# Two-pass P·V with the high and low parts of V side by side, in a two-layer mixer kernel

## The chip, the cores and the metric

The kernel runs on one core of one Trainium2 chip. The metric is the device time of one execution in microseconds (us); lower is better. The core's engines work side by side, each through its own queue in order, and wait for each other by semaphores: TensorE (PE in the profile, with its weight loads as PEld), VectorE (DVE), ScalarE (ACT), GpSimd (POOL) and SyncE (SP, which only issues DMAs here).

## The reference

Two layers work on 256 latent tokens (side x) and 256 context tokens (side c) of width 1024. Each layer has four attention branches A, B, C and D of 8 heads with head width 64, gated and merged, then a SwiGLU feed-forward part. What matters here is the last step of every attention:

```python
s = jnp.einsum('bqhgd,bkhd->bhgqk', qi, k, preferred_element_type=jnp.float32) * scale
p = jax.nn.softmax(s, axis=-1)
return jnp.einsum('bhgqk,bkhd->bqhgd', p.astype(v.dtype), v)
```

The latent queries look at 512 keys (latent and context), the context queries at the 256 context keys. All values are float32. The last layer needs no context output, so it has no side c queries. In every branch this step has the same form, o = P V, with P of 256 queries by 512 or 256 keys, V of that many keys by 64 columns.

## The kernel before

**Products in parts.** TensorE works with operands of a shortened type (fp32r). To keep float32 accuracy the kernel keeps each operand as a high part (the rounded value) and a low part (the value less its high part), and forms each product as three matmuls into the same sums, hi·hi, hi·lo and lo·hi. The helper `three` (lines L1605, L1606 and L1607 of the profile) does so for all of them; ScalarE makes the high part by a copy, VectorE the low part by a subtraction (GpSimd for some weights).

**The step list.** `build_plan` writes one list of steps, and every engine walks the same list and does its part of each step in that order. So the list sets the order of the work on every engine. Buffers are rings: `take` notes which signal frees a slot. Within an attention branch the list is made slot by slot. A slot belongs to one item, which is 128 queries of one head on side x, or all 256 of side c. `emit(k)` puts out the softmax of item k-1 ('den'), the turning of item k-2's probabilities by TensorE ('tr', L1790, PSUM to SBUF by 'trs': ScalarE L1279 for the high part, VectorE L1556 for the low part), and the scores of item k ('sc' in branch A, 'sc2' L1769 for a pair of heads in B, C and D; then 'mx', L1527 and L1534 on VectorE, and 'ex', L1271 on ScalarE). The reciprocal of a row sum is L1551 on VectorE and the scaled probabilities are L1142 on GpSimd.

**P·V.** `emit_pv(k)` puts out the steps 'pv' and 'ov' when a head's queries of one side are all turned: once for each head and side, so 64 times in layer 0 (32 heads, sides x and c) and 32 times in layer 1. 'pv' goes over four tiles of 128 keys (two on side c) and calls `three` for each, with 64 columns of V as the weights and 256 queries streaming, into partitions 0 to 63 of the one bank `pv_bank`. 'ov' empties it: ScalarE copies it to the high part of o (L1287), then VectorE subtracts to get the low part (L1560). The bank is free for the next 'pv' when the low part is there.

**What lies between.** The next unit's projections go into the same slots in small pieces: matmuls on a weight piece ('mm'), evacuation by ScalarE ('evac', L1231), rotary turning (TensorE L1720, GpSimd L1127, VectorE L1490 and L1494), splitting into parts ('qks', ScalarE L1239, VectorE L1500) and for V a turn by TensorE ('vtr', L1728) and its parts ('vs', ScalarE L1246, VectorE L1506). A filler of gate and branch products (evacuated by ScalarE, L1295, and VectorE, L1573) is spread over the slots by `levels`: every slot has a forced cost, `base_cost(k)`, counted in streamed columns, and gets filler up to a common level. `base_cost` counts a P·V at 12 times 256 columns on side x and 6 times 256 on side c. In layer 0 VectorE also works on the modulation vectors in those slots (L1381, four instructions in a row). Weight pieces are split into their parts four pieces ahead (ScalarE L1194; VectorE L1361 or GpSimd L1154).

**V in SBUF.** A generation of V takes two buffers of 512 columns a partition, the high part and then the low part. `v_places` gives where 'vs' writes them.

Of the kernel before, what the change touches and what calls it, by code (L numbers as in the profile page):

```python
# [29 lines left out]
P = 128  # L30
# [29 lines left out]
for _n, _w in (('ident', 128), ('ones', 1), ('power', 8), ('rotB', 128), ('rotA', 128), ('cosB', 256), ('sinB', 256),  # L60
# [38 lines left out]
    'sinksum': ('sum_ready',), 'den': ('rec_ready', 'prob_ready'),  # L99
    'tr': ('p_turned',), 'trs': ('pt_hi', 'pt_lo'), 'pv': ('pv_done',), 'ov': ('o_hi', 'o_lo'),  # L100
    'gsig': ('gate_tanh',), 'gmul': ('gate_mul',), 'gacc': ('gate_acc',), 'ms': ('m_hi', 'm_lo'),
# [101 lines left out]
def build_plan():  # L203
# [65 lines left out]
    for l in range(DEPTH):  # L269
# [292 lines left out]
        def base_cost(k):  # L562

            c = 0
            if k < len(items):
                both = items[k][0][1] != 'A'
                if not both or items[k][1] == first_head[items[k][0]]:
                    c += 3 * NTOK if items[k][2] == 'x' else 6 * CTX
            if 2 <= k < len(items) + 2:
                c += TURN  # L570
                if items[k - 2][2] == 'c' or items[k - 2][3] == 1:
                    c += 12 * SEQ if items[k - 2][2] == 'x' else 6 * SEQ
            return c
# [188 lines left out]
def build(nc, x, c, ctx, c_ctx, w_mod, b_mod, g_pre_mix, g_post_mix, g_pre_ffn, g_post_ffn, w_in, g_a_q, g_a_kv,  # L762
# [26 lines left out]
    with ExitStack() as es:  # L789
# [51 lines left out]

        mod_sums1 = flat[:, 0:2 * MOD_COLS].rearrange("p (s m) -> p s m", s=2)
        par = sb("par", [P, DEPTH, ROWS])
        sc = sb("sc", [P, 2, KT])
# [53 lines left out]
        def z(at, n=NTOK):  # L898
            return Z[:, at:at + n]
# [50 lines left out]
        def split_places(eng, key, f):  # L950
# [19 lines left out]
            return [(operand(ring, 0, gen, n), operand(ring, 1, gen, n), src)]  # L970

        def v_places(key, f, part):
            w = f['wide']
            dst = staged('V', f['dst'], part).rearrange("p (t w) -> p t w", t=4)[:, :, 0:w]
            return dst, acc(('vtr', key))[:, 0:4 * w].rearrange("p (t w) -> p t w", t=4)

# [11 lines left out]
        def o_places(g):  # L988
# [4 lines left out]
            t0 = 0 if side == 'x' else SEQ  # L993
            return (o_tile(0, i)[r0:r0 + DH, t0:t0 + SEQ], pv_bank[0:DH, 0:SEQ], o_tile(1, i)[r0:r0 + DH, t0:t0 + SEQ])

# [180 lines left out]
        def _(act):  # L1176
            for kind, key, f in steps:
# [102 lines left out]
                elif kind == 'ov':  # L1280
                    act.wait_ge(sem['pv_done'], count['pv_done', key])
                    if key[0][1:] in (('C', 0), ('D', 0)):

                        done = ('up', (key[0][0], KT - 1, 'CD'.index(key[0][1])))
                        act.wait_ge(sem['piece_used'], count['piece_used', (done, 0)])
                    dst, src, _ = o_places(key)
                    act.activation(dst, src, ACT.Copy).then_inc(sem['o_hi'], 1)  # L1287
                elif kind == 'gsig':
# [34 lines left out]
        def _(dve):  # L1323
            for kind, key, f in steps:
# [227 lines left out]
                elif kind == 'trs':  # L1552
# [3 lines left out]
                    dve.tensor_tensor(dst, src, hi.bitcast(F32), ALU.subtract).then_inc(sem['pt_lo'], 1)  # L1556
                elif kind == 'ov':
                    dve.wait_ge(sem['o_hi'], count['o_hi', key])
                    hi, src, lo = o_places(key)
                    dve.tensor_tensor(lo, src, hi.bitcast(F32), ALU.subtract).then_inc(sem['o_lo'], 1)  # L1560
                elif kind == 'gmul':
# [38 lines left out]
        def _(pe):  # L1600
# [8 lines left out]
            for kind, key, f in steps:  # L1609
# [182 lines left out]
                elif kind == 'pv':  # L1792
# [7 lines left out]
                    c0 = v_column(u, h)  # L1800
                    v = [staged('V', gen, a).rearrange("p (t w) -> p t w", t=4)[:, :, c0:c0 + DH] for a in range(2)]
                    tiles = range(4) if side == 'x' else range(2, 4)
                    for i, kt in enumerate(tiles):
                        ins = three(pv_bank[0:DH, 0:SEQ], [a[:, kt, :] for a in v],
                                    [pt(key, a)[:, i, :] for a in range(2)], i == 0, i == len(tiles) - 1)
                    ins.then_inc(sem['pv_done'], 1)
# [92 lines left out]
```

## Time and profile before

| what | value |
|---|---|
| time before, median of 3 runs | 2121.2 us (2120.85 to 2124.73) |
| profiled execution, its own time | 2117.97 us |
| profiled execution, span from first to last instruction | 2116.2 us |
| TensorE busy | 1899.1 us, 90% |
| VectorE busy | 1182.9 us, 56% |
| ScalarE busy | 865.7 us, 41% |
| GpSimd busy | 644.3 us, 30% |
| mean granted TensorE clock | 0.938 |

The profile comes from one execution, so its durations go with the time 2117.97 us, not with the median. A matmul's row has the time until its result is complete; matmuls are pipelined, so what a group of them costs is read from the distance between their starts. Idle time in brackets is that of the engine just before the instruction, with what ended it.

### The profile page before, as it was taken

How to read it: one execution, taken by the hardware profiler on the slowest of the kernel's cores; microseconds unless marked ns; L12 is line 12 of the kernel's file. 1: busy time of each engine (PE TensorE's matmuls, PEld its weight loads, DVE VectorE, ACT ScalarE, POOL GpSimd, SP SyncE). 2: the span in 40 equal slices, each digit the busy share in tenths (PEclk: the TensorE clock that was granted, in tenths of full speed). 3: DMA queues.
4: the chain of work that ended last, by engine and by line, in shares of the span. 5: the costliest groups of instructions: out<-in, count | busy, mean ns of one | idle time of the engine just before them, and what ended most of it. 6: DMA issues, size and time to landing. Idle time of an engine off the chain costs nothing. (4 is left out here: it accounts for less than half of the span.)

```text
span 2116.2 us, 32133 instructions
## 1 busy us (share of the span) xinstructions
PE 1899.1 (90%) x10899; PEld 1637.3 (77%) x10899; DVE 1182.9 (56%) x2360; ACT 865.7 (41%) x1870; POOL 644.3 (30%) x611
## 2 busy tenths in 40 slices
PE   8778899999988899968999999869999999979998
PEld 7566677777777777756777888757788888879997
DVE  6246666666556645268777522346564446645653
ACT  2245444444433443331222232246555545444453
POOL 6333343445444443020000100134435544311100
PEclk9989999999999999968999999779999999979998
DMA  7112333333332223215566433112344433435663
GB/s 280 53 49 60 82 85 96 95 90 108 88 84 65 70 57 122 72 60 154 174 187 193 128 95 97 45 37 64 81 120 101 115 81 91 115 95 164 183 183 109
DMA packets 391788, 223.69 MB, mean 106 GB/s; under 512 B 53398, under 2 KB 387532, under 8 KB 390604
## 3 DMA queue, kind: packets, MB, share of 16 engines
q1 hardware_dynamic: 389324, 218.50, 36.6%
q10 hardware_dynamic: 2304, 3.15, 0.5%
q8 instruction: 90, 1.47, 0.3%
q14 instruction: 70, 0.57, 0.1%
HBM read 218.44 MB, written 3.15 MB: 105 GB/s over the span
## 5 line engine op out<-in xcount | busy, mean ns | idle before, releaser
L1605 PE MATMUL bank<-Uhi,w_ring 128*128 128x512 f32 (+2 forms) x1664 | 604.7, 363 | 42.7 <-issue 27.1
L1606 PE MATMUL bank<-Ulo,w_ring 128*128 128x512 f32 (+2 forms) x1664 | 588.5, 354 | 0.0
L1607 PE MATMUL bank<-Uhi,w_ring 128*128 128x512 f32 (+2 forms) x1664 | 588.0, 353 | 0.0
L1361 DVE TENSOR_TENSOR w_ring<-load_ring,w_ring 128x512 fp32r<-128x512 f32 (+1 forms) x432 | 301.4, 722 | 260.1 <-ACT w_ring L1194 244.8
L1194 ACT ACTIVATE w_ring<-load_ring 128x512 fp32r<-128x512 f32 (+3 forms) x640 | 369.1, 603 | 85.2 <-PE bank L1607 74.6
L1605 PEld LDWEIGHTS bank<-Uhi,w_ring 128*128 128x128 f32 (+1 forms) x1664 | 327.1, 197 | 90.1 <-issue 32.3
L1154 POOL TENSOR_TENSOR w_ring<-load_ring,w_ring 128x512 fp32r<-128x512 f32 (+2 forms) x208 | 249.1, 1201 | 375.4 <-ACT w_ring L1194 237.7
L1607 PEld LDWEIGHTS bank<-Uhi,w_ring 128*128 128x128 f32 (+1 forms) x1664 | 326.3, 196 | 42.6
L1606 PEld LDWEIGHTS bank<-Ulo,w_ring 128*128 128x128 f32 (+1 forms) x1664 | 327.6, 197 | 36.6
L1605 PE MATMUL bank<-Z,w_ring 128*128 128x512 f32 (+2 forms) x784 | 275.6, 352 | 11.8 <-DVE Z L1500 6.1
L1606 PE MATMUL bank<-Z,w_ring 128*128 128x512 f32 (+2 forms) x784 | 269.5, 344 | 0.0
L1607 PE MATMUL bank<-Z,w_ring 128*128 128x512 f32 (+2 forms) x784 | 269.4, 344 | 0.0
L1142 POOL TENSOR_TENSOR Y<-Y,small 128x512 f32<-128x512 f32 x160 | 166.7, 1042 | 228.3 <-DVE small L1551 204.6
L1556 DVE TENSOR_TENSOR Z<-bank,Z 128x512 fp32r<-128x512 f32 x160 | 109.5, 684 | 129.9 <-ACT Z L1279 129.5
L1271 ACT ACTIVATE Y<-bank,small 128x512 f32<-128x512 f32 (+1 forms) x192 | 117.2, 612 | 142.8 <-DVE small L1534 142.5
L1605 PEld LDWEIGHTS bank<-Z,w_ring 128*128 128x128 f32 (+1 forms) x784 | 151.0, 193 | 31.2 <-issue 9.0
L1607 PEld LDWEIGHTS bank<-Z,w_ring 128*128 128x128 f32 (+1 forms) x784 | 151.1, 193 | 17.8 <-issue 0.3
L1606 PEld LDWEIGHTS bank<-Z,w_ring 128*128 128x128 f32 (+1 forms) x784 | 151.5, 193 | 16.3 <-issue 0.3
L1171 POOL TENSOR_TENSOR Z<-fil,Z 128x512 fp32r<-128x512 f32 (+1 forms) x44 | 45.0, 1024 | 384.1 <-ACT Z L1313 384.1
L1605 PE MATMUL bank<-Z 128*64 128x256 f32 (+2 forms) x368 | 112.1, 305 | 30.9 <-DVE Z L1500 23.4
L1381 DVE SCALAR_TENSOR_TENSOR tab<-Y,sc,tab 128x256 f32<-128x256 f32 x224 | 118.5, 549 | 34.1 <-DMA Y<-in_w_mod 27.9
L1279 ACT ACTIVATE Z<-bank 128x512 fp32r<-128x512 f32 x160 | 94.9, 593 | 85.3 <-PE bank L1790 83.0
(114 smaller groups left out, 2414.0 us busy)
## 6 DMA issues: line engine op xcount, KB each, us to landing
load_ring<-in_w_in SPq DMA_DIRECT2D x204, 256.0 KB, 3.0
load_ring<-in_w_ffn_in SPq DMA_DIRECT2D x176, 256.0 KB, 3.2
Y<-in_w_mod SPq DMA_DIRECT2D x96, 256.0 KB, 2.8
load_ring<-in_w_ffn_out SPq DMA_DIRECT2D x80, 256.0 KB, 3.1
mod_place<-in_w_mod SPq DMA_DIRECT2D x64, 256.0 KB, 2.8
load_ring<-in_w_branch SPq DMA_DIRECT2D x64, 256.0 KB, 2.9
mod_w<-in_w_mod SPq DMA_DIRECT2D x8, 1024.0 KB, 13.8
load_ring<-in_w_in SPq DMA_DIRECT2D x64, 128.0 KB, 2.6
```

The lines of the kernel that those rows point to most:

```text
L1142: pool.tensor_tensor(prob('Pn', key).rearrange("p (m k) -> p m k", m=m), prob('P', key).rearrange("p (m k) -> p m k", m=m), small[:, plan. ...
L1154: pool.tensor_tensor(w_ring[:, slot, 1, 0:sz], load_ring[:, plan.slot['load', key], 0:sz], w_ring[:, slot, 0, 0:sz].bitcast(F32), ALU.subt ...
L1171: pool.tensor_tensor(operand('hid', 1, key[1], n), fil[:, plan.slot['fil', ('ffn', key)], 0:n], operand('hid', 0, key[1], n).bitcast(F32), ...
L1194: act.activation(w_ring[:, plan.slot['w', key], 0, 0:sz], load_ring[:, plan.slot['load', key], 0:sz], ACT.Copy).then_inc(sem['w_hi'], 1)
L1271: ins = act.activation(prob('P', key)[:, a:b], s_bank(key)[:, a:b], ACT.Exp, bias=sm[:, 2 + i:3 + i], scale=scale_of(key), accum_out=sm[:, ...
L1279: act.activation(dst, src, ACT.Copy).then_inc(sem['pt_hi'], 1)
L1361: dve.tensor_tensor(w_ring[:, slot, 1, 0:sz], load_ring[:, plan.slot['load', key], 0:sz], w_ring[:, slot, 0, 0:sz].bitcast(F32), ALU.subtr ...
L1381: ins = dve.scalar_tensor_tensor(out=a, in0=w, scalar=by, in1=a, op0=ALU.mult, op1=ALU.add)
L1556: dve.tensor_tensor(dst, src, hi.bitcast(F32), ALU.subtract).then_inc(sem['pt_lo'], 1)
L1605: pe.matmul(dst, lhs[0], rhs[0], start=start, stop=False)
L1606: pe.matmul(dst, lhs[0], rhs[1], start=False, stop=False)
L1607: return pe.matmul(dst, lhs[1], rhs[0], start=False, stop=stop)
```

## The change

V's high and low part are put next to each other for every head and key tile: 64 columns of high part, then 64 columns of low part, in the same SBUF space. A P·V then takes two matmuls for a key tile instead of three: [V_hi | V_lo] as 128 columns of weights, with P_hi and then with P_lo streaming. Partitions 0 to 63 of the bank hold V_hi·P_hi + V_hi·P_lo, partitions 64 to 127 hold V_lo·P_hi + V_lo·P_lo (the last term was left out before). The step 'ov' now has four instructions: ScalarE copies partitions 64 to 127 of the bank to partitions 0 to 63 of a new buffer `o_raw`, VectorE adds partitions 0 to 63 of the bank to it, ScalarE copies the sum to the high part of o, VectorE subtracts for the low part. `base_cost` counts a P·V at 8 and 4 times 256 columns.

```diff
-    'tr': ('p_turned',), 'trs': ('pt_hi', 'pt_lo'), 'pv': ('pv_done',), 'ov': ('o_hi', 'o_lo'),
+    'tr': ('p_turned',), 'trs': ('pt_hi', 'pt_lo'), 'pv': ('pv_done',), 'ov': ('o_part', 'o_sum', 'o_hi', 'o_lo'),
...
-                    c += 12 * SEQ if items[k - 2][2] == 'x' else 6 * SEQ
+                    c += 8 * SEQ if items[k - 2][2] == 'x' else 4 * SEQ
...
+        def v_tile(gen, w):
+
+            return z(V_AT + 2 * plan.slot['V', gen] * NTOK, 8 * w).rearrange("p (t w) -> p t w", t=4)
+
         def v_places(key, f, part):
             w = f['wide']
-            dst = staged('V', f['dst'], part).rearrange("p (t w) -> p t w", t=4)[:, :, 0:w]
-            return dst, acc(('vtr', key))[:, 0:4 * w].rearrange("p (t w) -> p t w", t=4)
+            dst = v_tile(f['dst'], w).rearrange("p t (h a d) -> p t h a d", a=2, d=DH)[:, :, :, part, :]
+            return dst, acc(('vtr', key))[:, 0:4 * w].rearrange("p (t h d) -> p t h d", t=4, d=DH)
...
                 elif kind == 'ov':
                     act.wait_ge(sem['pv_done'], count['pv_done', key])
+                    if count['o_part', key] > 1:
+                        act.wait_ge(sem['o_lo'], count['o_lo', key] - 1)
+                    act.activation(o_raw[0:DH, :], pv_bank[DH:P, 0:SEQ], ACT.Copy).then_inc(sem['o_part'], 1)
+                    act.wait_ge(sem['o_sum'], count['o_sum', key])
...
-                    dst, src, _ = o_places(key)
-                    act.activation(dst, src, ACT.Copy).then_inc(sem['o_hi'], 1)
+                    act.activation(o_places(key)[0], o_raw[0:DH, :], ACT.Copy).then_inc(sem['o_hi'], 1)
...
                 elif kind == 'ov':
+                    dve.wait_ge(sem['o_part'], count['o_part', key])
+                    dve.tensor_tensor(o_raw[0:DH, :], pv_bank[0:DH, 0:SEQ], o_raw[0:DH, :],
+                                      ALU.add).then_inc(sem['o_sum'], 1)
                     dve.wait_ge(sem['o_hi'], count['o_hi', key])
-                    hi, src, lo = o_places(key)
-                    dve.tensor_tensor(lo, src, hi.bitcast(F32), ALU.subtract).then_inc(sem['o_lo'], 1)
+                    hi, lo = o_places(key)
+                    dve.tensor_tensor(lo, o_raw[0:DH, :], hi.bitcast(F32), ALU.subtract).then_inc(sem['o_lo'], 1)
...
-                    v = [staged('V', gen, a).rearrange("p (t w) -> p t w", t=4)[:, :, c0:c0 + DH] for a in range(2)]
+                    v = v_tile(gen, DH if u[1] == 'A' else P)
                     tiles = range(4) if side == 'x' else range(2, 4)
                     for i, kt in enumerate(tiles):
-                        ins = three(pv_bank[0:DH, 0:SEQ], [a[:, kt, :] for a in v],
-                                    [pt(key, a)[:, i, :] for a in range(2)], i == 0, i == len(tiles) - 1)
+                        for a in range(2):
+                            ins = pe.matmul(pv_bank[:, 0:SEQ], v[:, kt, 2 * c0:2 * c0 + P], pt(key, a)[:, i, :],
+                                            start=i == 0 and a == 0, stop=i == len(tiles) - 1 and a == 1)
```

## Rows read from the trace of the kernel before

**Rows 1.** Page, parts 1 and 2: busy time, and the granted clock in 40 slices.
```profile
PE 1899.1 (90%) x10899; PEld 1637.3 (77%) x10899; DVE 1182.9 (56%) x2360; ACT 865.7 (41%) x1870; POOL 644.3 (30%) x611
...
PEclk9989999999999999968999999779999999979998
```

**Rows 2.** Groups by form: count | busy us, mean ns | idle before, releaser.
```profile
L1605 PE MATMUL bank<-Z 128*64 128x256 f32 x320 | 90.8, 284 | 7.5 <-DVE Z L1556 7.4
```

**Rows 3.** Timeline of TensorE around one P·V of layer 1: start, duration, instruction.
```profile
1569.75 0.28 PE L1607 MATMUL bank<-Uhi,w_ring 128*128 128x256 f32 x1
1569.86 0.28 PE L1605 MATMUL bank<-Z 128*64 128x256 f32 x1
...
1571.24 0.60 PE L1790 MATMUL bank<-C,Y 128*128 128x128 f32 x4
```

**Rows 4.** Timeline of TensorE: first and last of twelve matmuls, 128 weight columns, 256 streamed.
```profile
1595.71 0.28 PE L1605 MATMUL bank<-Uhi,w_ring 128*128 128x256 f32 x1
...
1597.03 0.28 PE L1607 MATMUL bank<-Uhi,w_ring 128*128 128x256 f32 x1
```

**Rows 5.** Lines L1287 and L1560: duration min/median/max in ns; then L1560's wait (us, times).
```profile
L1287 ACT ACTIVATE Z<-bank x96: 361/377/379, 156.4 to 1833.3; 64x256 fp32r<-64x256 f32 x96
```
```profile
L1560 DVE TENSOR_TENSOR Z<-bank,Z x96: 406/417/420, 156.8 to 1833.7; 64x256 fp32r<-64x256 f32 x96
...
  ACT Z L1287: 128.8, 65
```

**Rows 6.** Timeline of one head of branch A in layer 1, ScalarE and VectorE.
```profile
1457.34 0.42 ACT L1239 ACTIVATE Z<-Y 96x256 fp32r<-96x256 f32 x1 [0.81 <-DVE Y L1494]
...
1457.89 0.42 DVE L1500 TENSOR_TENSOR Z<-Y,Z 96x256 fp32r<-96x256 f32 x1 [0.58 <-ACT Z L1239]
...
1458.34 0.42 DVE L1560 TENSOR_TENSOR Z<-bank,Z 64x256 fp32r<-64x256 f32 x1
...
1458.79 0.42 DVE L1506 TENSOR_TENSOR Z<-bank,Z 128x256 fp32r<-128x256 f32 x1
```

**Rows 7.** TensorE's waits from 140 to 830 us: total, times, longest.
```profile
PE bank L1605 <- DVE Z L1500: 18.8, 7, 4.4
PE bank L1769 <- DVE Z L1500: 12.5, 6, 3.4
PE bank L1720 <- ACT Y L1231: 8.5, 9, 1.3
...
PE bank L1728 <- ACT Y L1231: 3.4, 3, 1.7
```

**Rows 8.** TensorE's waits from 1436 to 1850 us.
```profile
PE bank L1720 <- ACT Y L1231: 5.2, 9, 1.1
PE bank L1605 <- DVE Z L1500: 4.6, 6, 0.9
```

**Rows 9.** Timeline behind one output evacuation in branch B of layer 0.
```profile
307.86 0.42 DVE L1560 TENSOR_TENSOR Z<-bank,Z 64x256 fp32r<-64x256 f32 x1 [1.15 <-ACT Z L1287]
...
308.38 0.59 ACT L1231 ACTIVATE Y<-bank 128x512 f32<-128x512 f32 x1
...
309.11 0.67 PE L1720 MATMUL bank<-Y,C 128*128 128x256 f32 x2 [1.26 <-ACT Y L1231]
```

**Rows 10.** Timeline where VectorE comes late to an output, branch C of layer 0.
```profile
438.73 0.38 ACT L1287 ACTIVATE Z<-bank 64x256 fp32r<-64x256 f32 x1
...
439.88 0.63 PE L1728 MATMUL bank<-C,Y 128*128 128x128 f32 x4 [1.66 <-ACT Y L1231]
...
440.31 0.42 DVE L1560 TENSOR_TENSOR Z<-bank,Z 64x256 fp32r<-64x256 f32 x1
```

**Rows 11.** Timeline at the end of layer 1's attention, two P·V 3.6 us apart.
```profile
1829.57 0.38 ACT L1287 ACTIVATE Z<-bank 64x256 fp32r<-64x256 f32 x1 [2.34 <-PE bank L1607]
...
1831.59 0.30 PE L1605 MATMUL bank<-Z 128*64 128x256 f32 x1 [0.19 <-DVE Z L1556]
```

**Rows 12.** Timeline: ScalarE's evacuation of turned probabilities, branch A of layer 1.
```profile
1462.63 0.60 ACT L1279 ACTIVATE Z<-bank 128x512 fp32r<-128x512 f32 x1 [0.17 <-PE bank L1790]
```

More of the change, by code:

```diff
@@ L842, in build @@
         mod_sums1 = flat[:, 0:2 * MOD_COLS].rearrange("p (s m) -> p s m", s=2)
+        o_raw = sb("o_raw", [P, SEQ])
         par = sb("par", [P, DEPTH, ROWS])
@@ L993, in o_places @@
             t0 = 0 if side == 'x' else SEQ
-            return (o_tile(0, i)[r0:r0 + DH, t0:t0 + SEQ], pv_bank[0:DH, 0:SEQ], o_tile(1, i)[r0:r0 + DH, t0:t0 + SEQ])
+            return o_tile(0, i)[r0:r0 + DH, t0:t0 + SEQ], o_tile(1, i)[r0:r0 + DH, t0:t0 + SEQ]
         block = es.enter_context(nc.Block())
```

## The prediction

> **What bounds the kernel now.** I read the page first, then the groups by form, then the waits of TensorE alone, and the timeline around the places that these named. The page shows TensorE busy 90% of a span of 2116.2 us, no other engine above 56%, and a granted clock of 0.9 or more over most of the attention of layer 0 (slices 3 to 15) and layer 1 (slices 27 to 34) [rows 1]. So the first look says: take work from TensorE. The second look is at where it stands still. Its waits in the attention of layer 0 are few and of one kind: it waits for a chain of ScalarE and VectorE that starts from a turned or projected tile (L1231, L1500) [rows 7], and the same kind returns in layer 1 [rows 8]. The reader should see that every link of these chains is an instruction of ScalarE or VectorE, and that the change puts two more of just those in the queue, 96 times over.
>
> **What TensorE is spared.** The three lines of the P·V have 320 matmuls each, 960 in all [rows 2]: 64 groups of 12 on side x and 32 groups of 6 on side c. Twelve of them take from 1569.86 to 1571.24, so 0.115 us a matmul from start to start, and the first starts 0.11 us after the matmul ahead of it [rows 3]. The changed group has 8 and 4 matmuls with 128 weight columns; the trace has no such P·V, but the same shape in the projections: eleven steps from 1595.71 to 1597.03, so 0.120 us each [rows 4]. I take that. A group of side x goes from 1.37 to 0.96 us, one of side c from 0.69 to 0.48: 0.41 and 0.21 us saved. In layer 0 that is 32 x 0.62 = 19.8 us, in layer 1 32 x 0.41 = 13.1 us, together 32.9 us. Bounds: at the old distance of 0.115 us it would be 320 x 0.115 = 36.8 us; if the wide weight load did not hide, it could not be worse than that of the projections, which have it already [rows 4].
>
> [...]
>
> **What the new chain costs.** Before, ScalarE copies (0.377 us) and VectorE subtracts (0.417 us) [rows 5]. Now ScalarE copies, VectorE adds, ScalarE copies from SBUF, VectorE subtracts. The bank copy keeps its 0.38 us. The add reads one operand from PSUM and one from SBUF as L1560 does: 0.42 us. The second copy reads SBUF like L1239 with 256 columns: 0.42 us [rows 6]. Each hand-over costs 0.03 us, as between rows of VectorE and ScalarE in the same stretch. So whatever is queued behind 'ov' on ScalarE comes 0.03 + 0.42 + 0.03 + 0.42 = 0.9 us later (I use 0.88), and so does what is queued behind it on VectorE. As work this is 96 x 0.8 = 77 us on two engines that are at 41% and 56% [rows 1], which by itself costs nothing. As delay it costs where TensorE waits for what is queued behind. Bounds for one output: 0 where there is slack, 0.88 us where there is none; over 96 outputs 0 to 84 us. Between them I go through the places.
>
> Layer 0, branch A. Behind the output of side c stand the copy of the turned probabilities (L1279) and the evacuation L1231, on which TensorE waits to rotate (L1720). Of its nine such waits [rows 7] seven start within 3 us behind an output: five in branch A, two in B. The pattern is output, L1279, L1231, and TensorE already idle for 1.26 us [rows 9]. Five times 0.88, once 0.6 where there was 0.25 us of slack, 0.7 at one P·V that comes straight behind, and 0.9 for VectorE's late arrival (below): 6.6 us. Branch B: two such waits, one wait for L1500 whose chain begins at an output, and one of 0.2: 2.8 us.
>
> Branch C of layer 0 has the dearest place. VectorE is in its four modulation instructions when ScalarE has the output ready: 1.58 us pass from 438.73 to 440.31 [rows 10]. So far ScalarE went on to L1231, and TensorE waited only for that. In the new order ScalarE stands until VectorE has added, so L1231 comes at 440.31 + 0.42 + 0.03 + 0.42 instead of 439.13: 2.1 us later. A like place about 43 us on has 0.8 us of slack and the same lateness: 1.4 us. One more plain case (the second of the three L1728 waits [rows 7]) adds 0.9. Sum 4.4 us. Branch D: three of the six waits of L1769 for L1500 [rows 7] start from an output that stands right ahead of the rotation on VectorE, and the last gate product waits behind the last output: 3.7 us. Layer 0: 6.6 + 2.8 + 4.4 + 3.7 = 17.5 us against 19.8.
>
> Layer 1, branch A. TensorE waits once a head for L1500 (six waits, 4.6 us) and for L1231 (six of the nine [rows 8]). The P·V runs in the shadow of that chain, so its 0.41 us a head are not gained: 7 x 0.41 = 2.9 us. The subtraction L1560 stands between L1500 and L1506 with no idle time [rows 6], so everything behind it moves; at the point where the loop goes back through TensorE, ScalarE has waited 0.17 us [rows 12], and in the head before 0.70. So 0.2 to 0.7 us of the 0.88 remain, 0.45 in the middle: 6 x 0.45 = 2.7 us. Branches B and C run dense; I find one place with no slack, 0.8 us. Branch D has two rotary or norm waits behind an output (1.8 us) and two P·V whose probabilities are copied by ScalarE right behind the output ahead [rows 11]: 0.8 each. Layer 1: 2.9 + 2.7 + 0.8 + 3.4 = 9.8 us against 13.1.
>
> **Moved without cost.** V's parts are written with the same element count in runs of 64, so L1246 and L1506 keep their time. The bank is released 0.9 us later; the nearest next P·V starts 3.4 us after the one before, 0.4 us more than the new group and chain need. No DMA is added. The new cost in `base_cost` moves a little filler (up to 1024 columns, a sixth of a piece) from slots without P·V to slots with one; this changes which stall has how much cover, in either direction, and I give it 3 us each way.
>
> **Sum.** 32.9 - 17.5 - 9.8 = 5.6 us gained. Against the profiled execution's 2118.0 us (span 2116.2 and 1.8 around it) that is 2112.4; that execution lies 3.2 us under the median of the runs, so the median forecast is 2121.2 - 5.6 = 2115.6 us.
>
> **The rivals.** (a) The delays fall into slack: the order shifts with every saved microsecond, and chains that are late now may not be. For it speaks that TensorE's waits behind outputs are under twenty of 96 outputs. Against it, that half of them have TensorE idle already. Keeping two thirds of the 27.3 us gives 2121.2 - 24 = 2097 at best, 2103 in the middle. Chance 0.15. (b) Slower: ScalarE parked behind VectorE. In layer 0 VectorE comes late to outputs in about twenty groups, by up to 2.5 us (some 16 us in sum, beyond the 0.41 that it needs anyway), and ScalarE's weight parts, gates and probabilities queue behind. I priced four of these. If all 16 us came through, and the added stalls dropped the granted clock twice (the slice around 132 us, with a stall of over 4 us, has 0.8 [rows 1]; 0.07 less in a slice of 52.9 us is some 7 us at 1.2 instead of 2.4 GHz, 3.5 us lost), the result is -5.6 + 12 + 7 = +13, 2134. It becomes slower than before when an output costs more than 32.9 / 96 = 0.34 us on average. Middle of this case 2128. Chance 0.23. (c) The saving is eaten to nothing: every P·V that TensorE finishes sooner only waits longer for the chain that feeds it, as in branch A of layer 1. Time within 4 us of before. Chance 0.17. (d) The change not doing what it says: the second pass would need separate weight loads for its two matmuls that do not hide; the projections exclude that [rows 4]. The forecast itself: 0.45, range 2110 to 2121.
>
> **How the numbers follow.** From the forecast case 0.27 lies under 2117 and 0.18 within 4.2 us of before; with (a) 0.42 faster by over 0.2%, with (c) 0.35 within 0.2%, and (b) gives 0.23 slower. 0.2% (4.2 us) is about what a measurement of this kernel can tell from no change. The range to hold 8 times in 10 reaches into (a) and (b): 2103 to 2128.
>
> **What would show it.** P·V groups of 8 and 4 matmuls 0.120 us apart, 0.96 us for side x. L1246 and L1506 unchanged. The copy of `o_raw` at 0.42 us. TensorE's waits for L1231 in layer 0 up by about 0.9 us each, the one near 440 us up by 2; heads of branch A in layer 1 9.5 us apart instead of 9.0. TensorE's idle time up by some 20 to 27 us while its matmul time is down by 33. I am wrong if the waits do not grow (then a), if new waits for L1194 or L1279 appear or the granted clock falls in slices 10 to 14 (then b), or if filler moved by the new cost opens or closes stalls that I have not listed.

## The result, and the profile after

The change makes the kernel slower: 2144.7 us median of 4 runs (2143.49 to 2150.46), against 2122.97 us for the kernel before in the same comparison (4 runs, 2120.85 to 2125.24). The ratio is 1.0108, 95% interval 1.0085 to 1.0131. The profiled execution has a span of 2141.8 us, 25.6 us more than before, and a mean granted clock of 0.931 instead of 0.938. Forecast were 2115.6 us and at most 2128.

The page of the kernel after, busy time and granted clock in 40 slices; the lines answer to [rows 1]:

```profile
PE 1881.2 (88%) x10579; PEld 1615.6 (75%) x10579; DVE 1222.9 (57%) x2456; ACT 907.0 (42%) x1966; POOL 640.3 (30%) x611
...
PEclk9989899999999999968999999779999999989998
```

There are 320 matmuls fewer, one instruction more per output on VectorE and on ScalarE (96 each), and TensorE is busy 17.9 us less. Yet the span grew. The clock row has a new 8 in the fifth slice (214 to 268 us); in the last slices one 7 became an 8.

The groups by form of the kernel after, the changed P·V; it answers to [rows 2], where each of three lines has 320:

```profile
L1816 PE MATMUL bank<-Z 128*128 128x256 f32 x640 | 94.0, 286 | 15.8 <-DVE Z L1564 15.5
```

The new instructions by tile, all uses of `o_raw`: duration min/median/max in ns, first and last start, then what their engines waited for (us, times). The old pair is in [rows 5]:

```profile
L1289 ACT ACTIVATE o_raw<-bank x96: 380/381/385, 151.8 to 1859.6; 64x256 f32<-64x256 f32 x96
L1567 DVE TENSOR_TENSOR o_raw<-bank,o_raw x96: 405/416/419, 152.2 to 1860.0; 64x256 f32<-64x256 f32 x96
L1295 ACT ACTIVATE Z<-o_raw x96: 414/417/419, 152.6 to 1860.4; 64x256 fp32r<-64x256 f32 x96
L1571 DVE TENSOR_TENSOR Z<-o_raw,Z x96: 416/421/511, 153.1 to 1860.9; 64x256 fp32r<-64x256 f32 x96
...
  DVE o_raw L1567: 64.6, 96
  ACT Z L1295: 46.3, 96
```

The four durations are the ones used in the forecast. The row to look at is the last but one: ScalarE stood idle for VectorE's add at all 96 outputs, 64.6 us. 96 adds of 0.45 us would be 43; the other 21 us are VectorE coming late. From the start of the first to the end of the last of an output's ScalarE instructions 141.2 us pass in sum, before 36.1 (96 x 0.376).

TensorE's waits from 140 to 830 us in the kernel after (total, times, longest), to be laid beside [rows 7]:

```profile
PE bank L1731 <- ACT Y L1236: 18.0, 10, 3.2
PE bank L1616 <- DVE Z L1508: 17.7, 7, 4.3
PE bank L1816 <- DVE Z L1564: 14.4, 8, 3.2
PE bank L1780 <- DVE Z L1508: 14.3, 6, 3.9
...
PE bank L1739 <- ACT Y L1236: 5.4, 3, 4.0
...
PE bank L1616 <- ACT H L1303: 2.0, 1, 2.0
```

The waits for the evacuation (L1231 before, L1236 now) went from 8.5 + 3.4 to 18.0 + 5.4 us; that is the foreseen kind. The P·V now waits 14.4 us for its own turned probabilities, and a projection waits 2.0 us for a gate (L1303). Both kinds are in the same view of the kernel before, where [rows 7] do not show them:

```profile
PE bank L1605 <- DVE Z L1556: 7.2, 3, 3.0
PE bank L1605 <- ACT H L1295: 1.1, 1, 1.1
```

The forecast read TensorE's waits as being of one kind. Of the first kind it priced one place in layer 0 (0.7 us), where 7.2 us were added.

Three places on the timeline of the kernel after (start, duration, instruction, idle before with its releaser). They answer to [rows 10], [rows 6] and [rows 3]:

```profile
440.04 2.88 DVE L1389 SCALAR_TENSOR_TENSOR mod_sums<-mod_place,sc,mod_sums 128x256 f32<-128x256 f32 x4
...
441.39 0.38 ACT L1289 ACTIVATE o_raw<-bank 64x256 f32<-64x256 f32 x1
442.84 0.41 DVE L1567 TENSOR_TENSOR o_raw<-bank,o_raw 64x256 f32<-64x256 f32 x1
443.28 0.41 ACT L1295 ACTIVATE Z<-o_raw 64x256 fp32r<-64x256 f32 x1 [1.51 <-DVE o_raw L1567]
443.72 0.60 ACT L1236 ACTIVATE Y<-bank 128x512 f32<-128x512 f32 x1
...
444.46 1.09 PE L1739 MATMUL bank<-C,Y 128*128 128x128 f32 x4 [3.96 <-ACT Y L1236]
...
1460.59 0.38 ACT L1289 ACTIVATE o_raw<-bank 64x256 f32<-64x256 f32 x1 [0.94 <-PE bank L1816]
1461.01 0.42 DVE L1567 TENSOR_TENSOR o_raw<-bank,o_raw 64x256 f32<-64x256 f32 x1 [0.76 <-ACT o_raw L1289]
1461.45 0.42 ACT L1295 ACTIVATE Z<-o_raw 64x256 fp32r<-64x256 f32 x1 [0.48 <-DVE o_raw L1567]
1461.78 0.40 ACT L1244 ACTIVATE Z<-Y 96x256 fp32r<-96x256 f32 x1
...
1462.31 0.42 DVE L1508 TENSOR_TENSOR Z<-Y,Z 96x256 fp32r<-96x256 f32 x1
...
1462.78 0.50 PE L1616 MATMUL bank<-Z 96*128 96x512 f32 x1 [1.79 <-DVE Z L1508]
...
1470.27 0.38 ACT L1289 ACTIVATE o_raw<-bank 64x256 f32<-64x256 f32 x1 [1.22 <-PE bank L1816]
...
1583.92 1.13 PE L1816 MATMUL bank<-Z 128*128 128x256 f32 x8
1584.89 0.60 PE L1801 MATMUL bank<-C,Y 128*128 128x128 f32 x4
```

The first place is the one that the forecast called the dearest. ScalarE has taken its part of the bank by 441.77, VectorE is in four modulation instructions until 442.84, and ScalarE stands for 1.51 us with the evacuation behind it; TensorE waits 3.96 us instead of 1.66. The second is a head of layer 1. Here something happened that the forecast had not: in [rows 6] the rotary copy (L1239) went ahead of the output; now it stands behind it (L1244 at 1461.78), and TensorE waits 1.79 us for what follows from it. Heads are 1470.27 - 1460.59 = 9.68 us apart. The third shows eight matmuls in 1584.89 - 1583.92 = 0.97 us.

**Where the time went.** Three sums over the whole trace close the account. The 96 P·V groups take 113.7 us before and 78.4 after: 35.3 saved. TensorE's idle time ahead of its instructions rose from 213.4 to 257.0 us: 43.6 more, of which 22.9 lie in the attention of layer 0, 18.8 in that of layer 1. The time lost to the lower of the two clock levels is (1 - mean granted clock) x span: 2116.2 x 0.062 = 131 and 2141.8 x 0.069 = 148 us, 17 more. -35.3 + 43.6 + 17 = +25.3, and the span shows +25.6. (Some 5 of the 17 us fall into stretches in which TensorE stands idle anyway, so they are counted twice; that the sum closes to 0.3 us is partly chance. The page alone gives the same in two terms: TensorE busy 17.9 us less, idle 43.6 us more.)

### The profile page after: what moved, and what is told of

It reads as the page before. It is cut to its first block and busy times, and to the rows that moved or that the text cites. A ratio compares the mean times of both kernels' runs of the same rounds, so it can differ in the third digit from the quotient of the medians.

```text
span 2141.8 us, 31780 instructions
## 1 busy us (share of the span) xinstructions
PE 1881.2 (88%) x10579; PEld 1615.6 (75%) x10579; DVE 1222.9 (57%) x2456; ACT 907.0 (42%) x1966; POOL 640.3 (30%) x611
## 5 line engine op out<-in xcount | busy, mean ns | idle before, releaser
L1618 PEld LDWEIGHTS bank<-Z,w_ring 128*128 128x128 f32 (+1 forms) x784 | 151.7, 193 | 18.2 <-issue 0.3
L1389 DVE SCALAR_TENSOR_TENSOR mod_sums<-mod_place,sc,mod_sums 128x256 f32<-128x256 f32 x224 | 121.9, 585 | 2.3
L1535 DVE TENSOR_REDUCE small<-bank 128x1 f32<-128x512 f32 x160 | 109.2, 683 | 20.5 <-PE bank L1618 15.0
## 6 DMA issues: line engine op xcount, KB each, us to landing
mod_w<-in_w_mod SPq DMA_DIRECT2D x8, 1024.0 KB, 13.6
```

The source lines that it names most:

```text
L1389: ins = dve.scalar_tensor_tensor(out=a, in0=w, scalar=by, in1=a, op0=ALU.mult, op1=ALU.add)
L1535: dve.tensor_reduce(sm[:, 0:m], s_bank(key)[:, :].rearrange("p (m k) -> p m k", m=m), AX_X, ALU.max).then_inc(sem['max_ready'], 1)
L1618: return pe.matmul(dst, lhs[1], rhs[0], start=False, stop=stop)
```

## The experiments

Each time is a median. Each ratio is to runs of the kernel before that were taken beside it (their medians lie between 2119.4 and 2121.9 us), with a 95% interval. Times of different experiments compare to within a few us.

**The two halves of the change, and its planner cost.** The first kernel is the change with the old cost of a P·V slot:

```diff
-                    c += 8 * SEQ if items[k - 2][2] == 'x' else 4 * SEQ
+                    c += 12 * SEQ if items[k - 2][2] == 'x' else 6 * SEQ
```

> The changed kernel with the slot planner's old cost of a P.V (12 and 6 times 256 columns). If the moved filler has a part in the loss, this lies over 4 us from the changed kernel's 2144.7 us, towards before. If the longer chain alone is the cause, it stays within 4 us of it: 2141 to 2149 us.

2154.39 us, 1.0162 (1.0149 to 1.0176): about 10 us slower than the change itself (1.0108). The new cost belongs to the two passes and is not what slows the kernel.

The second is the kernel before with nothing but the longer chain: three passes, then copy, VectorE's operation (a maximum of twice the same, which changes nothing), copy, subtraction.

```diff
-                    dst, src, _ = o_places(key)
-                    act.activation(dst, src, ACT.Copy).then_inc(sem['o_hi'], 1)
+                    act.activation(o_raw[0:DH, :], pv_bank[0:DH, 0:SEQ], ACT.Copy).then_inc(sem['o_part'], 1)
+                    act.wait_ge(sem['o_sum'], count['o_sum', key])
+                    act.activation(o_places(key)[0], o_raw[0:DH, :], ACT.Copy).then_inc(sem['o_hi'], 1)
...
+                    dve.wait_ge(sem['o_part'], count['o_part', key])
+                    dve.tensor_tensor(o_raw[0:DH, :], pv_bank[0:DH, 0:SEQ], o_raw[0:DH, :],
+                                      ALU.max).then_inc(sem['o_sum'], 1)
```

> The kernel before, three passes, with the change's four instructions to empty the bank (the copy and the bank hold the same sums and the add is a maximum, so the numbers stay those of before). Theory 1, the longer chain makes TensorE wait: before plus the 22 us of loss plus most of the 33 us of matmul time that is not saved here, 2165 to 2182 us. Theory 2, the change lost its time elsewhere (wide weights, the planner, V's layout): under 2135 us.

2177.15 us, 1.0263 (1.025 to 1.0276): 55 us for the chain alone. Its TensorE waits from 140 to 830 us:

```profile
PE bank L1612 <- DVE Z L1504: 17.3, 7, 4.3
PE bank L1727 <- ACT Y L1232: 16.6, 10, 3.0
PE bank L1776 <- DVE Z L1504: 14.6, 6, 4.2
PE bank L1612 <- DVE Z L1560: 12.9, 8, 2.8
```

The wait for the evacuation is twice that of [rows 7], and the P·V waits for the turned probabilities (last line) as in the changed kernel, so both come from the chain and not from the new P·V. The P·V's waits are 7.2 us before. Idle time grew by 35.1 us, the time lost to the clock from 131 to 157: together 61, the span grew by 58.9.

The third has the two passes and the old evacuation, of partitions 0 to 63 alone:

```diff
-                    act.activation(o_raw[0:DH, :], pv_bank[DH:P, 0:SEQ], ACT.Copy).then_inc(sem['o_part'], 1)
-                    act.wait_ge(sem['o_sum'], count['o_sum', key])
...
-                    act.activation(o_places(key)[0], o_raw[0:DH, :], ACT.Copy).then_inc(sem['o_hi'], 1)
+                    act.activation(o_places(key)[0], pv_bank[0:DH, 0:SEQ], ACT.Copy).then_inc(sem['o_hi'], 1)
```

> The changed kernel with two passes, but only partitions 0 to 63 of the bank are emptied, by the old two instructions; the product of V's low part is left out of the output. Theory 1: the matmuls' saving comes through except in branch A of layer 1, 2092 to 2105 us. If shorter P.V only makes TensorE wait longer for its chains: 2117 to 2124 us.

2096.18 us, 0.9881 (0.9865 to 0.9896): 25.7 us faster. Of 35.3 us of matmul time some 26 arrive; idle time is 8.1 us above that of before. (The profiled execution, the slowest of the four, is 19.7 us shorter than before: it also lost some 8 us more to the clock, 0.934 granted.) The two halves nearly add up: -25.7 + 55.3 = +29.6, the change shows +22.

**The shape of the chain.** The fourth keeps two passes but hands over once instead of three times: ScalarE copies the high part and then the other half of the bank, VectorE subtracts and then adds, and nobody on ScalarE waits for VectorE within an output.

```diff
+                    act.activation(o_places(key)[0], pv_bank[0:DH, 0:SEQ], ACT.Copy).then_inc(sem['o_hi'], 1)
+                    act.activation(o_raw[0:DH, :], pv_bank[DH:P, 0:SEQ], ACT.Copy).then_inc(sem['o_part'], 1)
...
+                    dve.tensor_tensor(o_raw[DH:P, :], pv_bank[0:DH, 0:SEQ], hi.bitcast(F32),
+                                      ALU.subtract).then_inc(sem['o_diff'], 1)
...
+                    dve.tensor_tensor(lo, o_raw[DH:P, :], o_raw[0:DH, :], ALU.add).then_inc(sem['o_lo'], 1)
```

> Two passes, but the halves are joined without a round trip: ScalarE copies partitions 0 to 63 as the high part and at once partitions 64 to 127 aside; VectorE subtracts the high part and adds the aside copy. ScalarE's queue is held 0.8 us instead of 1.3 and never waits for VectorE. If being parked behind VectorE and the round trip are the cause: 2108 to 2122 us. If it is the added work on the two engines (the same amount here): 2138 to 2148 us.

2120.62 us, 0.9988 (0.9972 to 1.0004; 12 runs, from 2105.92 to 2127.49). Four instructions of the same kinds without the round trip cost 24 us less than the change, and still 24 more than the passes alone.

The fifth splits the output in the queues. 'ov' is now ScalarE's part copy and VectorE's add, and frees the bank; a new step 'ow', high copy and subtraction, stands one slot later, ahead of that slot's exponential.

```diff
-    'tr': ('p_turned',), 'trs': ('pt_hi', 'pt_lo'), 'pv': ('pv_done',), 'ov': ('o_part', 'o_sum', 'o_hi', 'o_lo'),
+    'tr': ('p_turned',), 'trs': ('pt_hi', 'pt_lo'), 'pv': ('pv_done',), 'ov': ('o_part', 'o_sum'), 'ow': ('o_hi', 'o_lo'),
...
             emit(k)
+            if 3 <= k < len(items) + 3 and (items[k - 3][2] == 'c' or items[k - 3][3] == 1):
+                p.step('ow', items[k - 3][:3])
```

> The change with its four instructions, but the last two (copy to the high part, subtraction) are a step of their own that stands one slot later in the list; the bank is free after the add. ScalarE never stands waiting for VectorE behind the first copy. If the round trip and the parked ScalarE are the cause of the loss: 2105 to 2125 us. If the added work on the two engines is: 2138 to 2148 us.

2103.67 us, 0.9933 (0.9915 to 0.995; 6 runs, 2102.06 to 2111.98). This is 41 us under the change, with the same two passes and the same four operations; of the kernels that compute the whole output only the one with two buffers, further below, is as fast. On its timeline, the place that corresponds to the first one above, then a head of layer 1:

```profile
435.78 0.38 ACT L1291 ACTIVATE o_raw<-bank 64x256 f32<-64x256 f32 x1 [0.34 <-DVE Z L1575]
436.18 0.60 ACT L1238 ACTIVATE Y<-bank 128x512 f32<-128x512 f32 x1
...
437.43 0.41 DVE L1570 TENSOR_TENSOR o_raw<-bank,o_raw 64x256 f32<-64x256 f32 x1
...
1447.46 0.38 ACT L1291 ACTIVATE o_raw<-bank 64x256 f32<-64x256 f32 x1 [1.22 <-PE bank L1820]
...
1449.06 0.42 ACT L1298 ACTIVATE Z<-o_raw 64x256 fp32r<-64x256 f32 x1
...
1450.67 0.69 ACT L1278 ACTIVATE Y<-bank,small 128x512 f32<-128x512 f32 x1 [0.80 <-DVE small L1545]
...
1456.26 0.38 ACT L1291 ACTIVATE o_raw<-bank 64x256 f32<-64x256 f32 x1 [0.95 <-PE bank L1820]
```

VectorE is again late (437.43), but ScalarE went on to the evacuation at 436.18 at once. TensorE waits 2.34 us there, against 3.96 in the change. In layer 1 the high copy (L1298) lies in the gap in which ScalarE waits for the exponential's maximum anyway, and heads are 1456.26 - 1447.46 = 8.80 us apart, not 9.68. Idle time of TensorE is 222.0 us, as good as with the passes alone (221.5).

The sixth is the kernel before with the new planner cost alone (the first diff of this section, the other way round).

> The kernel before with nothing changed but the planner's cost of a P.V, 8 and 4 times 256 columns. Given back to the changed kernel, the old cost made it some 10 us slower. If the filler's new places are better whatever the P.V does: 2108 to 2116 us. If they only suit a shorter P.V: 2119 to 2130 us.

2117.16 us, 0.9992 (0.9979 to 1.0005): nothing that can be measured. It does make the rotary copy and the output change places in four heads of layer 1, as in the changed kernel. With an output of one ScalarE copy that is harmless.

The seventh moves the whole fork (both copies, subtraction, add) one slot later, and with it the release of the bank:

```diff
-                p.step('ov', g)
...
             emit(k)
+            if 3 <= k < len(items) + 3 and (items[k - 3][2] == 'c' or items[k - 3][3] == 1):
+                p.step('ov', items[k - 3][:3])
```

> The fork, with all of its instructions one slot later in the list, behind the next item's scores and maxima. Theory: what costs is that the output's emptying stands ahead of the probabilities' copy and the projections' evacuation in both queues, so moving it behind gives most of the saving back: 2092 to 2112 us. If the added work costs wherever it stands: 2116 to 2125 us, as the fork.

2133.21 us, 1.0065 (1.0048 to 1.0083), 13 us slower than the fork in place. Its TensorE waits have a new first line (140 to 1880 us):

```profile
PE bank L1819 <- DVE Z L1574: 29.8, 30, 5.0
```

Thirty P·V wait for the bank that the late add still reads. Delay is cheap only for the part that holds no bank.

The eighth adds no work instruction to the kernel before. ScalarE only waits behind each output copy until VectorE has subtracted:

```diff
                     act.activation(dst, src, ACT.Copy).then_inc(sem['o_hi'], 1)
+                    act.wait_ge(sem['o_lo'], count['o_lo', key])
```

> The kernel before with one wait more: behind its copy of the output ScalarE waits until VectorE has the low part, and no instruction is added. The wait lasts 0.45 us plus VectorE's lateness, 43 + 16 us over the 96 outputs. The longer chain cost 55 us for 105 us by which ScalarE's queue was held longer; at the same share this is 2145 to 2160 us. If a held ScalarE costs little and work is what counts: 2121 to 2130 us.

2145.04 us, 1.012 (1.0104 to 1.0137): 25 us for a bare wait. The dearest place again, on its timeline:

```profile
439.88 0.38 ACT L1287 ACTIVATE Z<-bank 64x256 fp32r<-64x256 f32 x1
441.45 0.42 DVE L1561 TENSOR_TENSOR Z<-bank,Z 64x256 fp32r<-64x256 f32 x1
441.90 0.60 ACT L1231 ACTIVATE Y<-bank 128x512 f32<-128x512 f32 x1 [1.65 <-DVE Z L1561]
442.64 0.78 PE L1729 MATMUL bank<-C,Y 128*128 128x128 f32 x4 [3.28 <-ACT Y L1231]
```

**The place in the queue.** Three more placements. The first has the split with 'ow' behind the exponential, right ahead of the next P·V's steps:

```diff
+            if 3 <= k < len(items) + 3 and (items[k - 3][2] == 'c' or items[k - 3][3] == 1):
+                p.step('ow', items[k - 3][:3])
             if 2 <= k < len(items) + 2 and (items[k - 2][2] == 'c' or items[k - 2][3] == 1):
```

> The split output as before, but its second step stands right ahead of the next P.V instead of ahead of the exponentials. If every instruction that stands ahead of the exponential costs: 2092 to 2101 us against the split's 2103.7. If the place hardly matters once the round trip is gone: 2100 to 2108 us. If ScalarE now meets a late VectorE again (the copy to the high part then stands right behind the exponential and ahead of the next output): over 2108 us.

2120.3 us, 1.0002 (0.9988 to 1.0017; 12 runs). The next leaves the fork in place and moves only VectorE's last add one slot later:

```diff
-    'tr': ('p_turned',), 'trs': ('pt_hi', 'pt_lo'), 'pv': ('pv_done',), 'ov': ('o_hi', 'o_part', 'o_diff', 'o_lo'),
+    'tr': ('p_turned',), 'trs': ('pt_hi', 'pt_lo'), 'pv': ('pv_done',), 'ov': ('o_hi', 'o_part', 'o_diff'), 'ow': ('o_lo',),
```

> The fork with only its last addition on VectorE moved one slot on; both copies of ScalarE and VectorE's subtraction stay at the old place, and the bank is free after them. The fork took 2120.6 us, 24 us over the passes alone, for 0.38 us more on ScalarE and 0.43 us more on VectorE. If VectorE's part makes the cost: 2098 to 2108 us. If ScalarE's copy ahead of the probabilities' copy makes it: 2114 to 2121 us.

2123.15 us, 1.0011 (0.999 to 1.0032; 12 runs), no better than the fork. The third has 'ow' at the very start of the slot, ahead of the step that turns the probabilities:

```diff
-            emit(k)
             if 3 <= k < len(items) + 3 and (items[k - 3][2] == 'c' or items[k - 3][3] == 1):
                 p.step('ow', items[k - 3][:3])
+            emit(k)
```

> The split with its second step at the very start of the slot, ahead of the reciprocal, the turn and the scores. The split won 41 us over the changed kernel and ScalarE's idle time ahead of the exponentials fell from 143 to 113 us. If the step is cheap because it fills that idle time: this place, ahead of the probabilities' copy, costs more, 2110 to 2125 us. If any place outside the P.V's own step will do: 2100 to 2108 us.

2133.86 us, 1.0055 (1.0039 to 1.0071). The same instructions in three places within one slot give 2103.7, 2120.3 and 2133.9 us. I first read this as free time ahead of the exponential: ScalarE's waits for VectorE's maximum there are 142.5 us in the kernel before, 110.3 in the split and 140.9 in the split behind the exponential. But each of the two slower placements also has a wait of its own. Behind the exponential, by ScalarE's waits (total, times, longest), the next output's part copy waits for the subtraction that still reads `o_raw`:

```profile
ACT o_raw L1291 <- DVE Z L1575: 50.1, 42, 2.8
```

At the start of the slot the high copy meets a VectorE that has not added yet, by the view of its line (count and duration, then what its engine waited for before it):

```profile
L1298 ACT ACTIVATE Z<-o_raw x96: 398/416/420, 155.5 to 1843.5; 64x256 fp32r<-64x256 f32 x96
...
  DVE o_raw L1570: 25.6, 44
```

In the split of the fifth experiment these two waits are 2.1 and 4.1 us. So the same placement behind the exponential was run with two buffers in turn:

```diff
-                    if count['o_part', key] > 1:
-                        act.wait_ge(sem['o_lo'], count['o_lo', key] - 1)
+                    if count['o_part', key] > 2:
+                        act.wait_ge(sem['o_lo'], count['o_lo', key] - 2)
```

> The split with the high copy and the subtraction behind the exponential, as in the run that gave 1.0002, but with two places for the sum that the outputs use in turn, so that the next output's part copy no longer waits for the subtraction of the one before (50.1 us, 42 times, in that run). If this wait is what separates it from the split ahead of the exponential (0.9933), the time falls to about 2105 us, 0.993. If what separates them is the free time ahead of the exponential, which this placement does not use, it stays at 2115 to 2121 us, 0.998 to 1.000.

2103.54 us, 0.9921 (0.9898 to 0.9943; 6 runs): level with the split ahead of the exponential. ScalarE's waits ahead of the exponentials are 138.5 us here, so the free time there goes unused and is not missed. My reading by free time falls. What separated these two placements was ScalarE standing for VectorE.

The old planner cost under the split:

> The split with the planner's old cost of a P.V. The changed kernel was 10 us slower with it, the kernel before only 2 us. If the filler's places have a part of their own that goes with two passes: 2109 to 2116 us against the split's 2103.7. If they only mattered beside the round trip: 2101 to 2107 us.

2113.53 us, 0.9958 (0.9943 to 0.9973), 10 us slower than the split with the new cost, as with the change itself.

**How much is VectorE's lateness?** Two kernels, before and after, in which the modulation accumulations of layer 0 (the four instructions behind which VectorE was late) cover 16 of 256 columns:

```diff
+                                if l == 0:
+                                    w, a = w[:, 0:16], a[:, 0:16]
```

> The kernel before, with VectorE's modulation sums of layer 0 accumulated over 16 of 256 columns only (the output's modulation terms are left incomplete). It takes away the four-instruction blocks that make VectorE late. Expected a few us to 20 us under before: 2100 to 2118 us. It is the base for the next kernel.

> The changed kernel with the same shortening of the modulation sums. If VectorE's lateness in layer 0 makes a large part of the loss, the change is at most 8 us slower than the shortened kernel before, or faster. If the round trip itself makes it, the difference stays at 18 to 26 us.

2109.42 us, 0.9939 (0.9917 to 0.9961), and 2131.95 us, 1.0047 (1.0027 to 1.0067). Each kernel gains, 11 and 13 us, and the distance between them stays: 22.5 us. In the changed kernel ScalarE's wait for the add fell from 64.6 to 50.4 us, so most of VectorE's lateness was gone. The long blocks of VectorE are costly for both and are not the cause of the difference.

**One instruction each.** The kernel before with one more ScalarE copy behind every output copy, and the kernel before with one more VectorE addition ahead of every subtraction; nothing reads either:

```diff
+                    act.activation(o_raw[0:DH, :], const('cosB', DH), ACT.Copy)
```

```diff
+                    dve.tensor_tensor(o_raw[0:DH, :], src, hi.bitcast(F32), ALU.add)
```

> The kernel before with one copy more on ScalarE right behind each of the 96 output copies, 64 partitions by 256 columns from SBUF, about 0.42 us; nothing reads it and nothing waits. The fork added 0.38 us on ScalarE and 0.42 on VectorE and cost 24 us over the passes alone. If ScalarE's queue makes that cost: 2136 to 2146 us. If VectorE's does: 2120 to 2126 us.

> The kernel before with one addition more on VectorE ahead of each of the 96 subtractions, of the same shape, about 0.42 us; nothing reads it. If ScalarE's queue makes the cost: 2118 to 2128 us. If VectorE's queue does: 2136 to 2146 us.

2124.49 us, 1.002 (1.001 to 1.003; 12 runs): 4 us for 40 us of ScalarE work. 2136.64 us, 1.0067 (1.005 to 1.0083): 16 us for 40 us of VectorE work. Then both at once, still with no wait between the engines:

> The kernel before with both extra instructions at once, ScalarE's copy behind each output copy (alone 1.002) and VectorE's addition ahead of each subtraction (alone 1.0067), and no wait between the engines. If the two costs add up, 1.009, 2139 us; the long chain's 55 us would then be 20 of work and 35 of waiting for each other. If they compound, 1.015 or more, 2152 us, and the round trip is worth less than the bare wait's 25 us.

2132.73 us, 1.0059 (1.004 to 1.0078; 6 runs), 13 us over its kernel before (2119.36, 11 runs). Both together cost no more than VectorE's alone. The long chain has instructions of the same kinds and durations per output and costs 55 us; the 42 us between are the price of the engines' waiting for each other, the bank's later release included. TensorE's waits from 140 to 830 us, here with both instructions added and no hand-over:

```profile
PE bank L1609 <- DVE Z L1503: 18.7, 7, 4.3
PE bank L1773 <- DVE Z L1503: 13.3, 6, 3.8
PE bank L1724 <- ACT Y L1233: 10.0, 9, 1.4
...
PE bank L1609 <- DVE Z L1559: 6.2, 4, 2.4
```

The third line is 16.6 us in the long chain and 8.5 before [rows 7], the last 12.9 us in the long chain and 7.2 before.

## Why the prediction was wrong

**The step that failed is the sum of the chain's delays: 24.4 us were priced, 55 measured.** That is the long chain alone; in the changed kernel it is 2144.7 - 2096.2 = 48.5 us over the passes alone. The mechanism was the one named (four instructions that wait for each other in place of two, work behind them later on both queues, TensorE waiting for that). Its size was half of what it is, and it lies in the hand-overs: instructions of the same kinds without them cost 13 us. The shortfall has two parts. In the long chain's profiled execution TensorE is idle 35.1 us more, where 24.4 were priced, and busy 23.9 us more with the same matmuls, at a mean granted clock of 0.928 instead of 0.938, a term that the forecast put at nothing without a reason. Point by point:

- **TensorE's saving, 32.9 us: right.** The groups shrank by 35.3 us, at 0.12 us a matmul. 25.7 us reach the end with the old evacuation; the forecast let 2.9 be hidden.
- **Duration of each new instruction: right** (0.381, 0.416, 0.417, 0.421 us against 0.38, 0.42, 0.42, 0.42), and so is the 0.88 us where VectorE is on time: 0.45 + 0.45.
- **Idle time: 27 us foreseen at most, 43.6 found.** By stage, forecast against found: layer 0, A 6.6 and 7.7, B 2.8 and 5.4, C 4.4 and 6.3, D 3.7 and 3.5; layer 1, A 5.6 (with the hidden savings) and 6.9, B and C together 0.8 and 6.2, D 3.4 and 5.7. Where TensorE already waited for the evacuation, the count was good: 5.0 + 1.8 + 4.4 = 11.2 us priced in layer 0, 11.5 found. Missing are the P·V waiting for its probabilities (15.5 us where [rows 2] have 7.4: a wait that was in the trace and was read over but for 0.7 us in layer 0 and 1.6 in layer 1), the gates (L1303: 7.6 us, L1295 before: 4.7), and the dense branches B and C of layer 1, where the forecast had found one place only. Since the P·V's waits lie in the same stages, the close match by stage in layer 0 is in part luck. I had priced one kind of stall; a delay of 0.9 us or more at 96 places also lengthens the others and makes new ones.
- **The clock: nothing foreseen, 17 us lost.** Only the slower rival had a term for it, 7 us for two falls of the clock. The account (idle + 16, clock + 17, saving + 2 in the kernel's favour) gives the 31 us between the forecast -5.6 and the 25.6 found. It is an account, not an experiment: no run here held the idle time and moved the clock alone.
- **The planner's cost, 3 us either way: mis-sized.** It is worth 10 us, in favour, once the passes are two (two pairs of kernels), and nothing in the kernel before. Inside that gain it also put the output ahead of the rotary copy in layer 1, which made heads 9.68 us apart where 9.5 were forecast from the old order; with the old cost and the old order the change has heads 9.3 to 9.6 us apart.
- **The place near 440 us: right.** 2.1 us later was forecast, TensorE waits 3.96 us instead of 1.66.
- **Signs of being wrong.** New waits behind the copy of the probabilities came, as named for the slower rival. The granted clock fell in slice 5, not in slices 10 to 14 as named. V's parts kept their time (medians 384 and 425 ns before, 383 and 425 after), as forecast.

**The rivals.** Rival (b), slower, is what happened, and with more than its price: 2128 to 2134 were given, 2144.7 came. Its threshold, 0.34 us an output, was passed with 48.5 / 96 = 0.51. Its first part, ScalarE held by VectorE, is shown: a bare wait costs 25 us, and a second buffer that removes 50.1 us of such waits from the split gives 17 us back. Its emphasis on VectorE's modulation blocks is not: with them cut short the difference is the same. Rival (a), in which the delays fall into slack, is excluded by the long chain alone. Rival (c), in which a shorter P·V only waits longer, and (d), in which the second pass does not do what it says, are excluded by the passes alone, of whose 35.3 us some 26 arrive.

**What stays open.** The bare wait costs 25 us, the hand-overs of the long chain some 42; which of its three carries the rest was not isolated. The fork has no wait of ScalarE for VectorE within an output and is still 24 us over the passes alone, where the work alone should cost about 13; moving its last add gained nothing. The split at the start of the slot was not run with the wait for the add removed, so that this wait makes it slow is only argued. Some kernels (the fork, the split behind the exponential, the late add) spread over 11 to 25 us from run to run; their place near 1.000 is sure, an order among them is not. And the shares of stall and clock in any of these costs are an account only.

## What to carry to other kernels

Work added to ScalarE and VectorE is cheap while they have slack (13 us for 80 us of it); hand-overs inside one step of an in-order queue are not (about 42 us for the round trip, 25 us for a bare wait), and they must also be priced where nothing waits yet, since the stalls counted in the trace came to 24 of 55 us. Split such a step: let the first half free the bank, put the second half where its input is long ready (that this matters is argued from waits, not isolated), and give it a buffer that the next output does not wait for (this is shown); the two passes then give 2103.7 us (0.9933) ahead of the exponential with one buffer, or 2103.5 (0.9921) behind it with two, where the change as made gives 2144.7 (1.0108). Then change the planner's cost with the work: it is worth 10 us with two passes and nothing without.

## What the runs showed of the hardware

- Four instructions an output in place of two cost 13 us without hand-overs, with them 55; the same four of the change, split, give 2103.7, 2120.3 or 2133.9 us by place in one slot, and the middle one falls to 2103.5 with a second buffer.
- In branch C of layer 0 (from the end of its first exponential to that of branch D's) the long chain added 8.0 us of idle time (15.2 to 23.2) but 16.7 us of span (199.3 to 216.0); the time at 1.2 GHz there rose from 13.6 to 31.7 us. With the bare wait it was 6.0 us of idle and 11.8 us of span, and 28.5 us at 1.2 GHz. Around that stage of the long chain the granted clock fell 0.2 to 1.3 us behind the end of pauses of TensorE of 3.6, 1.9 and 2.2 us. By the Trainium skill, page "TensorE: Matmul & The Clock Gate", section "HAM oscillation — how this bites in real kernels", pauses of TensorE put its clock back to the lower level. The trace agrees in kind. If the whole loss is put down to the added stalls, they cost up to twice their length; but the sum of the stalls does not set the clock: with the extra VectorE addition alone the same stage has 0.2 us more idle time, 5.8 us more span and 24.2 us at 1.2 GHz.
- An extra VectorE addition of 0.42 us at 96 places made TensorE's idle time only 6.6 us longer, and yet the span grew by 18.2; the time lost to the clock grew by 12. Why the clock fell more often there is open.
